# Mixer turn of a hybrid RG-LRU and neighbourhood-attention block: values stationary, softmax in one pass, gate matmuls in pieces inside attention, norms in two chunks, the next turn's input computed early

## What is computed

```
xr, kx, vx, gx, qx, mrx, mnx = jnp.split(xn @ w_in[l], list(IN_SPLITS), axis=-1)
cr, kc, vc = jnp.split(cn @ w_in[l][:, :CTX_KV_COLS], [D_RNN, D_RNN + D_ATT], axis=-1)
xr = dwconv(xr, lru_conv_w[l], lru_conv_b[l], LRU_CONV_LEFT)
cr = dwconv(cr, lru_conv_w[l], lru_conv_b[l], LRU_CONV_LEFT)
h_x, h_c = rglru_bidirectional(xr, cr, ...)
y_rnn_x = h_x * jax.nn.gelu(gx)
qx, kx, kc = head_rms(qx, ...), head_rms(kx, ...), head_rms(kc, ...)
y_na_x = neighborhood_attention(rope_2d(qx), qx, rope_2d(kx), vx, kc, vc, na_rpb[l])
x = x + mx[2] * merge_branches(y_rnn_x, y_na_x, mrx, mnx, ...)
x = x + mx[5] * conv_ffn(modulate(x, ...), ...)
```

## Time and profile before

| | us |
|---|---|
| median of 3 runs | 2500.17 |
| lowest, highest | 2495.57, 2503.16 |
| span of the profiled execution | 2496.4 |

### The profile page before, as it was taken

The page is one execution under the profiler, slowest core; times in us unless marked ns, Lnnn a source line. Parts: engine busy times, 40 slices in busy tenths (PEclk is TensorE's granted clock), DMA queues, the critical chain, the costliest instruction groups (busy, mean ns, idle before and its releaser), DMA issues. The chain is left out here.

```text
span 2496.4 us, 33475 instructions
## 1 busy us (share of the span) xinstructions
PE 2283.0 (91%) x11706; PEld 1963.8 (79%) x11706; DVE 1463.6 (59%) x2860; ACT 1021.2 (41%) x1782; POOL 138.3 (6%) x147
## 2 busy tenths in 40 slices
PE   5398999989989989989899879999799999999999
PEld 4387878878878878789688768888588888888887
DVE  7657468477486584784764764565655324533452
ACT  3366466465564674664656541110322112211220
POOL 4000000101001001000000000000000000000000
PEclk9698998989999999989999889999899999999999
DMA  6411110211012001111110235442222111111112
GB/s 237 125 41 43 54 47 19 66 43 48 24 43 54 30 30 54 47 35 49 43 54 9 71 117 202 151 142 101 69 76 76 51 42 51 50 51 51 50 51 93
DMA packets 66793, 167.90 MB, mean 67 GB/s; under 512 B 22497, under 2 KB 23777, under 8 KB 66529
## 3 DMA queue, kind: packets, MB, share of 16 engines
q1 hardware_dynamic: 45648, 145.13, 17.3%
q0 software_dynamic: 4608, 16.78, 2.0%
q10 hardware_dynamic: 16400, 4.19, 0.8%
HBM read 145.11 MB, written 25.17 MB: 68 GB/s over the span
## 5 line engine op out<-in xcount | busy, mean ns | idle before, releaser
L48 PE MATMUL f_ps<-xnh,fh 128*128 128x512 f32 (+1 forms) x512 | 204.5, 399 | 73.6 <-DVE fl L920 52.5
L686 PE MATMUL o_ps<-vS,probTH 128*128 128x128 f32 (+1 forms) x832 | 216.3, 293 | 7.3 <-DVE probTL L1071 7.3
L48 PE MATMUL q_ps<-qh,xnh 128*128 128x384 f32 (+1 forms) x640 | 220.6, 345 | 0.0
L50 PE MATMUL q_ps<-qh,xnl 128*128 128x384 f32 (+1 forms) x640 | 208.0, 325 | 0.0
L49 PE MATMUL q_ps<-ql,xnh 128*128 128x384 f32 (+1 forms) x640 | 207.9, 325 | 0.0
L686 PE MATMUL o_ps<-vS,probTL 128*128 128x128 f32 (+1 forms) x832 | 206.2, 282 | 0.0
L49 PE MATMUL f_ps<-xnl,fh 128*128 128x512 f32 (+1 forms) x512 | 200.7, 392 | 0.0
L50 PE MATMUL f_ps<-xnh,fl 128*128 128x512 f32 (+1 forms) x512 | 200.1, 391 | 0.0
L48 PEld LDWEIGHTS f_ps<-xnh,fh 128*128 128x128 f32 x512 | 104.3, 204 | 100.3 <-issue 73.1
L686 PEld LDWEIGHTS o_ps<-vS,probTH 128*128 128x128 f32 (+1 forms) x832 | 163.5, 197 | 17.4 <-DVE probTL L1071 8.3
L686 PEld LDWEIGHTS o_ps<-vS,probTL 128*128 128x128 f32 (+1 forms) x832 | 164.6, 198 | 0.0
(11 more groups left out here) (301 smaller groups left out, 5733.3 us busy)
## 6 DMA issues: line engine op xcount, KB each, us to landing
raw_d<-w_ff SPq DMA_DIRECT2D x68, 512.0 KB, 3.2
raw<-w_fm SPq DMA_DIRECT2D x32, 512.0 KB, 4.2
raw<-w_qkv SPq DMA_DIRECT2D x24, 512.0 KB, 3.8
raw_c<-w_mix SPq DMA_DIRECT2D x24, 512.0 KB, 4.2
rows_c<-w_modT SPq DMA_DIRECT2D x24, 512.0 KB, 3.3
bias<-bias_d SPq DMA_DIRECT2D x16, 448.0 KB, 7.1
wm<-w_mod SPq DMA_DIRECT2D x8, 512.0 KB, 8.9
xs<-xT SPq DMA_DIRECT2D x8, 512.0 KB, 8.9
```

Of the source, the lines that this page charges most:

```text
L48: pe.matmul(out, w_hi(k), x_hi(k), start=(k == 0), stop=False)
L50: last = pe.matmul(out, w_lo(k), x_hi(k), start=False, stop=(k == chunks - 1))
L686: last = pe.matmul(out, probT[part][u % 2][0:keys, b, :], vS[0:keys, tile, h, :], start=(b == 0 and part == 0), stop=(b == 6 and part == 1))
```

## The change

On PE, a turn now starts with G; then come the ten tiles (the two context tiles first) with the recurrence's gates after tiles 0 to 2 and 4 to 6; then XR **of the next turn**, MR, and attention. MN is cut into its eight chunks of the contraction for each segment (`piece`, three matmuls of 512 columns), two chunks in every even step. XR of turn 0 is computed ahead of the first turn. In the last turn MN is whole and there is no XR.

In attention two steps with the same head and neighbouring query tiles form a pair (a group). The value halves (128 keys x 128) are now the stationary operand and the transposed probabilities of **both** steps the moving one (256 columns, 128 at the edges of the window): 12 matmuls in an outer pair and 16 in an inner one. They stand in the odd step, behind the transposes of that same step. The output comes out transposed, so the transposes of the output are gone; its upper and lower halves are added after ACT has copied one half across partitions (`bottoms`), and the inverse of the softmax sum is spread by two transposes of a broadcast column. The softmax takes window and context in one exponential of 768 or 896 columns, from a minimum of negated scores in two reductions. Norm, rotation and transposes run in two chunks of tiles; the inverse root is a `pow` on POOL. The branch gates use tanh on ACT with two operations on POOL in place of the sigmoid. POOL adds the masks in three operations with 256, 896 and 1792 columns. The weights `w_fm` are laid out per turn.

```diff
-RAW_SLOT = [0, 1, 2, 0, 1, 2, 1]
+F_G, F_GATES, F_XR, F_MR, F_MN = 0, 2, 14, 17, 19
+GROUPS_ATT = ATT // 2
+CHUNKS = ((0, 2 + NT // 2), (2 + NT // 2, Q_TILES))
...
                 def weighted_values(i, g):
...
+                    pe.wait_ge(inverted, i * ATT + 2 * g + 2)
+                    for e in (1, 0):
+                        pe.transpose(O_ps[:, 384 - P * e:512 - P * e],
+                                     stat[:, 2 * g + e, 3:4].broadcast_to([P, P]), ident)
+                    pe.wait_ge(pt_lo, i * (2 * ATT) + 4 * g + 4)
...
+                            last = pe.matmul(dst, vS[:, s, h, :], moving, start=(n == 0 and part == 0),
+                                             stop=(n == len(blocks) - 1 and part == 1))
+                    last.then_inc(pv_done, 1)
...
+                    for u in range(ATT):
+                        prob_transposes(i, u)
+                        if not last and u % 2 == 0:
+                            piece()
+                        if u + 2 < ATT:
+                            scores(i, u + 2)
+                        if not last and u % 2 == 0:
+                            piece()
+                        if u % 2 == 1:
+                            weighted_values(i, u // 2)
...
                 def soft(i, u):
+                    p = prob[u % 3][:, (0 if is_inner(u) else P):14 * GW]
+                    act.wait_ge(bound_done, i * ATT + u + 1)
+                    act.activation(p, p, ACT.Exp, bias=stat[:, u, 1:2], scale=-1.0,
+                                   accum_out=stat[:, u, 2:3]).then_inc(exp_done, 1)
...
+                def bottoms(i, g):
+                    rows, others = HEAD_ROWS[g % 2], HEAD_ROWS[1 - g % 2]
+                    act.wait_ge(pv_done, i * GROUPS_ATT + g + 1)
+                    act.wait_ge(y_done, i * GROUPS_ATT + (g - 1 if g else 0))
+                    act.copy(bot[rows, :], O_ps[others, 0:256]).then_inc(bottom, 1)
...
+                    pool.tensor_tensor(rstd[:, 1, s0:s1, :], v, power[:, :].unsqueeze(1).broadcast_to(v.shape), ALU.pow)\
+                        .then_inc(rms_root, 1)
...
+                    for u in range(ATT):
+                        probT_low(i, u)
+                        inverse(i, u)
+                        if u + 2 < ATT:
+                            maxima(i, u + 2)
+                        if u % 2 == 0 and u >= 2:
+                            outputs(i, u // 2 - 1, first)
```

More of the change, by code:

```diff
@@ L455, in _ @@
[L455 to L469 removed]
+                sp.wait_ge(w_lo, 1)
@@ new lines, in f_evac, with q_evac @@
+                    return act.activation(out, f_bank(j)[:, 0:out.shape[1]], func, **kw).then_inc(f_free, 1)
+                def q_evac(i, s, first=False):
+                    w0 = P if s < NCT else 0
+                    act.wait_ge(q_full, i * Q_TILES + s + 1)
+                    act.copy(qkv[:, s, w0:384], q_banks[s % 3][:, w0:384])
+                    if s >= 2:
+                        act.wait_ge(sq_used, i * Q_TILES + s - 1)
+                    elif s == 0 and not first:
+                        for n in range(2):
+                            act.wait_ge(yn_out[n], i * 32)
+                    act.activation(sqs[:, s % 2, w0:256], q_banks[s % 3][:, w0:256], ACT.Square).then_inc(q_free, 1)
@@ new lines, in turn @@
+                    for s in range(3):
+                        q_evac(i, s, first)
+                        gate_pieces(i, *GATES_AFTER[s])
+                    decays(i, 0)
+                    q_evac(i, 3)
+                    q_evac(i, 4)
+                    root(i, 0)
+                    gate_pieces(i, *GATES_AFTER[4])
+                    q_evac(i, 5)
+                    gate_pieces(i, *GATES_AFTER[5])
+                    if not last:
+                        split_hi(XR, raw_count(XR, i))
@@ L895, in turn @@
                     soft(i, 0)
                     soft(i, 1)
+                    tr_high(i, JOBS_B)
+                    if last:
+                        act.wait_ge(stage_out, i * 64 + 48)
+                        act.wait_ge(f_full, f_count(i, LAST_MN + 1))
+                        act.activation(stage[:, :], F_ps[:, :], ACT.Tanh, scale=0.5).then_inc(f_free, 1)
+                    else:
+                        branch(i, F_MR + 1, 1, first)
                     for u in range(ATT):
+                        if u % 2 == 0 and u >= 2:
+                            bottoms(i, u // 2 - 1)
@@ L1143, in turn @@
-                    head_norm(i, 0, NT, gqk[:, 0, :])
-                    complement(i, 1)
+                    for s in range(4):
+                        head_squares(i, s)
+                    gated_input(i, 0)
+                    complement(i, 0)
+                    head_squares(i, 4)
+                    scan(i, 0)
+                    head_squares(i, 5)
+                    if not last:
+                        split_low(XR, i)
+                    inverse_roots(i, 0)
+                    head_norm(1, *CHUNKS[0])
```

1107 lines of the change are left out of this document (607 added, 500 removed).

## The result

| | before | after |
|---|---|---|
| median, us | 2499.74 | 2564.61 |
| lowest, highest | 2495.57, 2503.16 | 2560.56, 2572.82 |
| span of the profiled execution | 2496.4 | 2558.7 |

After to before is 1.0268, with a 95% interval of 1.0252 to 1.0284: the change costs 65 us. The forecast was 2534, in a range of 2440 to 2595: the sign is right, and some 31 us are missing.

What follows compares the result with a forecast made beforehand. PE bounds, with DVE right behind; attention waits on a chain across PE, DVE and ACT. +15 (turn 0), 6 x 4.8 (middle turns) and -10 (turn 7) make +34 us on 2500.2: 2534 us, range 2440 to 2595.

Steps and rivals of the forecast that it cites:

- the sign: Whole kernel: slower than before, with chance 0.52, against 0.36 for faster and 0.12 for the same.
- The chain in attention: Attention: values wait on a chain through PE, DVE and ACT; pairs 9.3 us inner, 8.1 outer, 69 us a turn.
- The width: Attention's value matmuls: 256 columns cost the same 0.12 us as 128, and half as many are wanted.
- Rival (4): Value matmuls: 256 columns take twice the 128-column time, 8 x 1.7 us more a turn, 2640 us; chance 0.02.
- The clock: Attention: in two of three pairs a 3.4 us stretch falls to 1.2 GHz, 9 us a turn, ends 0 and 14.
- The head: From a turn's last values to the next first transposes of probabilities: 97 us, where it was 117.6.
- The `pow`: Head: POOL's two inverse-root operations stand on DVE's path, allowed 0 to 2 us each, with no row.
- the convolution: Head, on DVE: 6.7 us, with 1 us of PE wait before the gates, or 5 if slowed beside the masks.
- rival (3): Head: DVE and POOL later (slow `pow`, convolution beside masks, MR's single bank), 6 us more a turn, 2580 us; chance 0.14.
- Turn 0: First turn, with its own XR and turn 1's: 174 us, or 183 with low clock; 167.9 before.
- Turn 7: Last turn, no pieces or next XR, recurrent splits on the chain: attention 76, head 97, together 173 us; 182.8 before.
- Rival (1): Attention: same chain but the clock holds, no stretch at 1.2 GHz; 30 us less, 2470 us; chance 0.27.

Runs made afterwards that it cites:

- e4_filled: The changed kernel with 16 idle matmuls more in each pair, right ahead of PE's wait for the inverse before L804: 2522.2 us.
- e2_copies_first: The changed kernel with ACT's order alone changed, the odd step's high copies ahead of the exponential of step e+2: 2486.2 us.
- e11_head_only: The changed kernel with DVE work moved into its waits for `pow` and POOL's masks held back until the convolution is done, attention as in the change: 2516.2 us.
- e10_start: The kernel with both head edits and reordered attention (2403.7 us), plus DVE's first XR and G splits ahead of the norm-weight scaling: 2396.1 us.
- e6_under_pow: The changed kernel with the XR weight split and the first chunk's low parts moved into DVE's waits for `pow` in the head: 2538.9 us.

## Why the prediction was right in sign and 31 us short

**The chain in attention: right.** Inner pairs of 9.3 us were forecast. The one shown takes 9.14, and 9.07 with its wait filled; the four of turn 4 take 10.8, 9.1, 9.4 and 8.6 in e4_filled, the first of them with the G split in it. Attention at full clock 69 and 69.3. The waits before L804 averaged 2.2 us over all 64 pairs and came from DVE's reciprocal. PE's own work was 7.0. That the exponential ahead of the high copies makes the chain was shown by e2_copies_first, which changes only that. Inside the 69, the G split (about 1.1 us) was missing, and the other terms were too high by as much: there the sum came out right by luck.

**The width: right.** 0.12 us for 256 columns. Rival (4) is out.

**The clock: right mechanism, too dear.** 9 us a turn were taken, 6.1 are shown by e4_filled, inside the ends of 0 and 14. Over six middle turns and turn 0 this was some 20 us too much, and it hid part of the error below. That is luck: with the measured clock the forecast would have been about 2514, 51 us short and not 31.

**The head: this step failed.** 97 us were forecast for the head of each turn. Measured are 105.0, 102.1, 104.5, 101.5 and 103.0 ahead of turns 2 to 6, 96.3 ahead of turn 1 and 100.5 ahead of turn 7. Two terms were mis-sized. The `pow` was allowed "0 to 2 us each" without a row; its two operations in a turn took 4.17 and 2.89, and DVE waited 4.3 and 3.0 for them in a middle turn, 58.4 us in all. And the convolution was put at 6.7 us, its meeting with the masks priced only as a wait of PE (1 us, with 5 as the other end). It took 8.8 or 12.5, on DVE's list, which the forecast itself had ending last in the head. The low clock behind waits in the head, past the turn's start, was in no term either. e11_head_only takes out both and finds the head at 97. So rival (3), which named these two causes, holds for the head at nearly its full size: it had 6 us a turn, the heads ahead of turns 2 to 6 were 6.2 over the 97, those ahead of turn 1 0.7 below and of turn 7 3.5 over, and e11_head_only gave back 48 us. The kernel stayed under its 2580 mostly because the clock had been taken too dear. Its third cause, MR's single bank, shows in no wait.

**Turn 0: 10 us too short.** 183 were forecast, 192.8 measured. 6.1 of them are the first matmul, which came at 108.1 where it came at 102.0 before. I took the beginning of turn 0 as given, though the change puts the weights of XR and G ahead of the norm weights among the first loads and leaves DVE's scaling of these in front of its splits. e10_start shows that nothing but this order held PE up. The runs that leave this order alone show that start at 104.2 to 107.3, so of the 6.1 it is 2 to 5 in other executions. From there to the first transposes it took 110.9 us, where the forecast had 105; in e6_under_pow this stretch is 3.7 shorter, which is the part of `pow`. The other 2.2 stay open. Against them stands the clock term, 2.4 too high here.

**Turn 7: 176.5 instead of 173**, with attention at 75.9 as forecast (76) and the head 3.5 longer. But the 76 was right by luck: it was 72 of chain and 4 of clock, and with the waits filled (e4_filled) this attention still took 75.7 us, at a granted clock of 0.95. There the splits of the recurrent branch cost more than I counted.

Together: +10 for turn 0, 6 x 2.6 for the middle turns and +3.5 make 29 of the 31 us. (Rival (1) takes 11 us off turn 7, where its own terms, 97 + 72 against 182.8, give 14; this changes no reading.)

## What to carry to other kernels

When a change makes one engine's list shorter, walk the chain that a step must pass through the other engines' lists, in their order, before counting the gain: here PE's list shrank as planned and the kernel lost 65 us, until two lines of ACT's order gave back 78. A wait is paid for twice where it also lowers PE's clock, so harmless work placed in it can pay: 1024 idle matmuls gave 42 us. The table of waits shows what one engine lost at one line and not what a slower operation costs its own engine's list: 10.4 us in the table were 24 in the kernel. And an operation that has no row in the trace needs a wide bound, most of all if another engine stands still for it.

## What the runs showed of the hardware

- `pow` on POOL is very slow by element: 24 columns took 4.17 us and 16 columns 2.89, 0.17 to 0.18 us a column, where an addition of 512 columns on POOL took 1.04 us.
- 16 idle matmuls of 0.12 us in each pair raised the granted clock in attention from 0.89 to 1.00 and cut 42 us.
- Behind PE waits of 2.1 to 2.7 us in attention the clock was at its lower level in many pairs (0.51 in the stretch behind the wait of 2.66 us), though not in each: the pair at 959.12 has a wait of 2.13 us and stayed at 1.00.
- DVE's convolution and POOL's masks side by side: 9.68 instead of 3.92 us for the three long operations of the one, and for the longest operation of the other 4.90 instead of 4.04.
